# Channel mixer: weight halves meet paired columns of 512, sample tokens by gathered expert rows, lower halves of the down tiles on VectorE

## What is computed

```python
def block(xb):
    q = (xb @ w_q).reshape(blk, PEER_HEADS, 2, PEER_HALF)
    s = jnp.einsum('thcd,chkd->thck', q, sub_keys).astype(F32)
    sv, si = lax.top_k(s, PEER_TOPK)
    cand = (sv[:, :, 0, :, None] + sv[:, :, 1, None, :]).reshape(...)
    top_s, ci = lax.top_k(cand, PEER_TOPK)
    ...
    e = i1 * PEER_KEYS + i2
    gate = jax.nn.softmax(top_s, axis=-1)
    act = jax.nn.gelu(jnp.einsum('thed,td->the', u[e], xb), approximate=False)
    return jnp.einsum('the,thed->td', (gate * act), v[e])
```

## Time and profile before

| | |
|---|---|
| median of 3 runs | 2504.04 us |
| profiled execution, its span | 2507.1 us |
| first channel mixer, first to last product | 404.0 to 1268.6 us |
| second channel mixer | 1628.5 to 2493.5 us |
| TensorE busy in the span | 2330.1 us (93%) |
| VectorE, ScalarE, GpSimd busy | 1713.6, 1112.0, 1669.8 us |
| mean granted TensorE clock | 0.958 |

### The profile page before, as it was taken

How to read it: one execution, slowest core, us unless ns; L and a number is a source line. 1 busy time by engine, 2 the same in 40 slices (tenths; PEclk the granted TensorE clock), 3 DMA queues, 4 the chain that set the end, 5 groups by cost and what they waited for, 6 DMA issues and landing times. The chain is left out here.

```text
span 2507.1 us, 46304 instructions
## 1 busy us (share of the span) xinstructions
PE 2330.1 (93%) x19024; PEld 2217.5 (88%) x19024; DVE 1713.6 (68%) x2773; ACT 1112.0 (44%) x1893; POOL 1669.8 (67%) x716
## 2 busy tenths in 40 slices
PE   6977978999999999999979875899999999999998
PEld 5957858999999999999979722899999999999998
DVE  4776553795678268888868376349767762888887
ACT  4512234455554444444446412344555444444443
POOL 4714016687666788888867544758766668888885
PEclk9978988999999999999989977899999999999999
DMA  4410013454444555555535443445544445555553
GB/s 156 153 52 34 35 44 135 144 185 160 144 144 144 169 184 178 184 178 184 179 123 169 157 151 109 133 137 163 176 146 147 145 147 182 180 182 181 181 182 131
DMA packets 102226, 370.27 MB, mean 148 GB/s; under 512 B 15392, under 2 KB 15744, under 8 KB 98816
## 3 DMA queue, kind: packets, MB, share of 16 engines
q1 hardware_dynamic: 102016, 367.30, 45.4%
HBM read 352.67 MB, written 14.58 MB: 146 GB/s over the span
## 5 line engine op out<-in xcount | busy, mean ns | idle before, releaser
L355 POOL TENSOR_TENSOR weights_halves<-weights_raw,weights_halves 128x1024 fp32r<-128x1024 f32 x638 | 1541.6, 2419 | 571.1 <-ACT weights_halves L347 570.8
L347 ACT CAST weights_halves<-weights_raw 128x1024 fp32r<-128x1024 f32 x638 | 669.9, 1051 | 936.2 <-PE peer L378 482.6
L860 DVE TENSOR_TENSOR gated<-acts,gated 128x264 fp32r<-128x264 f32 x256 | 615.3, 2405 | 127.5 <-ACT gated L742 127.5
L378 PE MATMUL peer<-ffn_in_hi,weights_halves 128*128 128x264 f32 x4608 | 650.7, 288 | 14.9 <-ACT ffn_in_hi L271 14.9
L378 PEld LDWEIGHTS peer<-ffn_in_hi,weights_halves 128*128 128x128 f32 x4608 | 590.9, 189 | 22.0 <-issue 16.6
L364 PE MATMUL peer<-gated,weights_halves 128*128 128x264 f32 x2048 | 583.2, 285 | 0.0
L362 PE MATMUL peer<-gated,weights_halves 128*128 128x264 f32 x2048 | 581.2, 284 | 0.0
L363 PE MATMUL peer<-gated,weights_halves 128*128 128x264 f32 x2048 | 579.9, 283 | 0.0
L363 PEld LDWEIGHTS peer<-gated,weights_halves 128*128 128x128 f32 x2048 | 385.9, 188 | 0.0
L362 PEld LDWEIGHTS peer<-gated,weights_halves 128*128 128x128 f32 x2048 | 385.4, 188 | 0.0
L364 PEld LDWEIGHTS peer<-gated,weights_halves 128*128 128x128 f32 x2048 | 384.4, 188 | 0.0
(11 more groups left out here) (465 smaller groups left out, 2359.3 us busy)
## 6 DMA issues: line engine op xcount, KB each, us to landing
weights_raw<-in_up SPq DMA_DIRECT2D x256, 512.0 KB, 3.5
weights_raw<-in_down SPq DMA_DIRECT2D x256, 512.0 KB, 3.5
weights_raw<-in_ssm_w_in SPq DMA_DIRECT2D x40, 512.0 KB, 3.4
weights_raw<-in_w_q SPq DMA_DIRECT2D x32, 512.0 KB, 3.4
weights_raw<-in_ab_w_in SPq DMA_DIRECT2D x30, 512.0 KB, 3.5
weights_raw<-in_ssm_w_out SPq DMA_DIRECT2D x16, 512.0 KB, 3.5
states<-in_ssm_in SPq DMA_DIRECT2D x8, 1024.0 KB, 7.4
ssm_sample<-states SPq DMA_DIRECT2D x8, 1024.0 KB, 4.8
```

The costliest lines, as they stand in the source:

```text
L347: act.copy(self.halves[:, 0, slot, :], self.raw[:, slot, :]).then_inc(self.hi_made, 1)
L355: pool.tensor_tensor(self.halves[:, 1, slot, :], self.raw[:, slot, :], self.halves[:, 0, slot, :].bitcast(F32), ALU.subtract).then_inc(sel ...
L378: ins = pe.matmul(out, self.halves[:, half, n % RING, at], both[side], start=start and half == 0 and side == 0 and k == 0, stop=stop and h ...
L860: core.gated_lo.inc(dve.tensor_tensor(a_lo[:, j % RING, :], acts[:, j, :], a_hi[:, j % RING, :].bitcast(F32), ALU.subtract))
```

## The change

**512 paired columns.** The 8 sample tokens leave the up and down products, so 256 columns are left. Upper and lower token halves lie side by side (`pairs` in SBUF, `a_pairs` in the ring of gated tokens). In a down tile, and in an up tile from 40 on, an upper weight block meets all 512 columns in one matmul, and a lower one meets the 256 columns of the upper tokens and adds to the second half of the bank: 16 matmuls instead of 24. The two halves of the bank are added when they leave it: in up tiles ScalarE copies the second half to `cross`, VectorE adds it in the bank, and then comes the GELU; in down tiles VectorE adds both to `x`. Up tiles 0 to 39 keep 24 matmuls, of 256 columns. SP fills `pairs` by two DMAs from SBUF to SBUF behind the norm.

**Quads.** 64 quads instead of 66, spread over the 84 tiles 40 to 123 (`QUAD_AT`), in runs of three or four tiles with one tile between.

**Samples.** Expert numbers and gates of the samples are put on 128 rows (8 tokens x 16), one column per head. GpSimd gathers, head by head, the 128 rows of `u` (a new input `up_rows`) and then of `v` by indirect DMA into three slots. VectorE takes the dot product with the sample's row (`dot`), ScalarE one GELU, VectorE sums the weighted rows (`weigh`), all within the down tiles, one step every six tiles. 8 matmuls then sum 16 rows to a token, within the last tile.

**Lower halves.** Those of the down tiles are made by VectorE (`make_lo_on_dve`) instead of GpSimd.

```diff
+    def pair_product(self, pe, out, n, cols, pair, start, stop):
         hi, lo = self.halves[:, 0, n % RING, cols], self.halves[:, 1, n % RING, cols]
-        pe.matmul(out, hi, rhs_hi, start=start, stop=False, skip_group_check=True)
-        pe.matmul(out, hi, rhs_lo, start=False, stop=False, skip_group_check=True)
-        return pe.matmul(out, lo, rhs_hi, start=False, stop=stop, skip_group_check=True)
+        pe.matmul(out, hi, pair, start=start, stop=False, skip_group_check=True)
+        return pe.matmul(out[:, SEQ:2 * SEQ], lo, pair[:, 0:SEQ], start=False, stop=stop, skip_group_check=True)
...
-QUADS = T // 4
-EXP_TILE = 22
-TURN_TILE = 36
-FIRST_GATED = 38
-GATED_AHEAD = 120
+QUADS = SEQ // 4
+EXP_TILE = 24
+TURN_TILE = 38
+FIRST_GATED = 40
+FIRST_PAIRED = FIRST_GATED
+QUAD_TILES = 84
+GATED_AHEAD = 124
+FIRST_DOT = 10
+FIRST_WEIGHTED = 64
+SAMPLE_STEP = 6
+SAMPLES_AFTER = 3
...
@@ SP
                 core.load(sp, keys, sub_keys)
+                sp.wait_ge(core.norm_hi.sem, norm.hi0 + KC)
+                halves_paired.inc(sp.dma_start(pairs[:, :, 0:SEQ].bitcast(F32),
+                                                    h_hi[:, :, 0:SEQ].bitcast(F32)), 16)
+                sp.wait_ge(core.norm_lo_pool.sem, norm.pool0 + KC // 2)
+                sp.wait_ge(core.norm_lo_dve.sem, norm.dve0 + KC // 2)
+                halves_paired.inc(sp.dma_start(pairs[:, :, SEQ:2 * SEQ].bitcast(F32),
+                                                    h_lo[:, :, 0:SEQ].bitcast(F32)), 16)
                 ring.load_to(sp, end + RING)
@@ GpSimd
+                ring.make_lo(pool, down)
+                pool.wait_ge(core.sample_copied.sem, kinds0 + 1)
+                pool.wait_ge(ring.multiplied, down)
+                for n in range(2 * PEER_HEADS):
+                    if n >= GATHER_SLOTS:
+                        pool.wait_ge(gather_used.sem, used0 + n - GATHER_SLOTS + 1)
+                    head = n % PEER_HEADS
+                    gathered[n % GATHER_SLOTS].inc(pool.indirect_dma_start(...), 16)
                 ring.make_lo(pool, end + RING)
@@ TensorE
+                    if s == 0:
+                        pe.wait_ge(rows_copied.sem, rows_copied0 + 1)
+                        for k in range(KC):
+                            last = pe.matmul(row_banks[k // 4][:, (k % 4) * P:(k % 4 + 1) * P],
+                                             sample_rows[:, k * P:(k + 1) * P], core.ident, start=True, stop=True)
...
+                        if j == KEYS - 1 and d == SAMPLES_AFTER:
+                            pe.wait_ge(cross_added.sem, crossed0 + 4)
+                            pe.wait_ge(gather_used.sem, used0 + 2 * PEER_HEADS)
+                            for k in range(KC):
+                                summed = pe.matmul(sums[1][:, k * DEC:(k + 1) * DEC], weighted_sum[:, columns[k]],
+                                                   core.row_token, start=True, stop=True)
@@ ScalarE
                     act.wait_ge(ring.multiplied, up + j + 1)
+                    if j >= FIRST_PAIRED:
+                        cross_copied.inc(act.copy(cross, bank[:, SEQ:2 * SEQ]))
+                        ring.make_hi(act, up + j + RING + 1)
+                        act.wait_ge(halves_added.sem, added0 + j - FIRST_PAIRED + 1)
@@ VectorE
+                def add_halves(j):
+                    dve.wait_ge(cross_copied.sem, copied_cross0 + j - FIRST_PAIRED + 1)
+                    bank = projected[(SETS + j) % RING]
+                    halves_added.inc(dve.tensor_tensor(bank[:, 0:SEQ], bank[:, 0:SEQ], cross, ALU.add))
...
                 for j in range(FIRST_GATED, KEYS):
+                    quad = QUAD_AT.get(j)
+                    if j >= FIRST_PAIRED:
+                        add_halves(j)
+                    if j > FIRST_GATED:
                         gate_tile(j)
+                    if quad is not None:
+                        apply(quad, j)
+                        if quad + 2 < QUADS:
+                            build(quad + 2)
...
+                for j in range(KEYS):
+                    if j + RING < KEYS:
+                        ring.make_lo_on_dve(dve, down + j + RING)
+                        make_gated_lo(j + RING)
+                    if j >= FIRST_DOT and (j - FIRST_DOT) % SAMPLE_STEP == 0 and (j - FIRST_DOT) // SAMPLE_STEP < PEER_HEADS:
+                        dot((j - FIRST_DOT) // SAMPLE_STEP)
...
+                    add_to_x(dve.tensor_tensor(x[:, d, 0:SEQ], sums[d][:, SEQ:2 * SEQ], x[:, d, 0:SEQ], ALU.add))
+                    last = dve.tensor_tensor(x[:, d, 0:SEQ], sums[d][:, 0:SEQ], x[:, d, 0:SEQ], ALU.add)
```

More of the change, by code:

```diff
@@ L21 @@
 SSM_SLOTS = 3
+GATHER_SLOTS = 3
 class Count:
@@ L158, in _ @@
                 dve.tensor_reduce(core.sample_head, eye.rearrange("p (h t) -> p h t", t=DEC), AX_X, ALU.add)
+            dve.tensor_reduce(core.row_token, core.ident.rearrange("p (t k) -> p t k", k=TOPK), AX_X, ALU.add)
+    with nc.Block() as block:
+        @block.vector
+        def _(dve):
+            dve.tensor_scalar(core.sample_head_up, core.sample_head, float(KEYS), None, ALU.mult)
 SUM_BANK = 3
@@ L651, in score @@
                     core.head_scored.inc(last)
-                def tile_product(tile, out):
-                    ring.products(pe, out, tile, [(h_hi[:, k, :], h_lo[:, k, :]) for k in range(KC)],
-                                  [slice(k * P, (k + 1) * P) for k in range(KC)], start=True,
-                                  stop=True, norm=norm if tile == first else None).then_inc(ring.multiplied, 1)
+                columns = [slice(k * P, (k + 1) * P) for k in range(KC)]
                 for s in range(SETS):
@@ L672, in _ @@
                         pe.wait_ge(core.tile_gated.sem, gated0 + j - RING - FIRST_GATED)
-                    tile_product(up + j, projected[bank][:, 0:T])
+                    if j == 0:
+                        pe.wait_ge(halves_paired.sem, paired0 + 32)
+                    if j < FIRST_PAIRED:
+                        last = ring.products(pe, projected[bank][:, 0:SEQ], up + j,
+                                             [(pairs[:, k, 0:SEQ], pairs[:, k, SEQ:2 * SEQ]) for k in range(KC)],
+                                             columns, start=True, stop=True)
+                    else:
+                        last = ring.pair_products(pe, projected[bank][:, :], up + j,
+                                                  [pairs[:, k, :] for k in range(KC)], columns)
+                    last.then_inc(ring.multiplied, 1)
                     if j == 0:
@@ L2847, in program @@
             sources += [d[name][n] for n in tiles]
-        core.ring = Ring(core, ctx, sources)
+        on_dve = {first[name] + j for name in ("down0", "down1") for j in range(KEYS)}
+        core.ring = Ring(core, ctx, sources, on_dve)
         with nc.Block() as block:
```

226 lines of the change are left out of this document (159 added, 67 removed).

## The result

The changed kernel takes 2463.5 us (median of 4 runs, 2462.8 to 2466.1); before, on the same chips, 2506.2. The ratio is 0.9832, its 95% interval 0.9818 to 0.9846: 42.7 us faster, where 74 were forecast. The time lies within the range on record (2400 to 2474), and outside the likeliest case's own range (2408 to 2450).

What follows compares the result with a forecast made beforehand. TensorE was taken as the bound, through the distance between matmul starts. Tile and quad savings of -96 us, +8 for the round, +13 for mixer starts and ends and +1 summed to -74: 2430 us, range 2400 to 2474.

Steps and rivals of the forecast that it cites:

- likeliest case: Whole kernel: TensorE sets the pace throughout, 2430 us, own range 2408 to 2450; chance 0.52.
- the hidden loads: Rival, paired tiles: all weight loads hide, a tile takes 2.62 us, the whole 2410 or 2403; chance 0.08.
- the round: Paired up tiles: VectorE and ScalarE waiting on each other, about 3.85 us a tile with a quad; term +8 us (0 to +40).
- tiles of 2.8 us without a wait: Paired tiles: sign that the working is wrong and the matmul's loss grows with its columns.
- the price of the 512-column matmul: Paired up and down tiles: 0.216 us, of which 0.213 is columns; with a 256-column matmul 0.337 a pair.
- Down tiles: 256 down tiles in both mixers, from 2.915 to 2.70 us each: -55 us (-22 to -76).
- Paired up tiles: 176 up tiles, 40 to 127 of both mixers, from 2.90 to 2.70 us each: -35 us (-12 to -49).
- Start and end of the mixers: Each mixer: sample-row matmuls 1.8 us, a late weight load 0.5, its end 4.4; +13 us for both.
- The loss goes with the columns: Rival, paired tiles: the matmul's loss scales with columns, a tile takes 2.83 us, the whole 2480; chance 0.10.
- The round sets the up tiles: Rival, paired up tiles: VectorE and ScalarE's chain binds; 2454 us at 0.3 us more a round, 2479 at 0.5; chance 0.25.
- Lower halves take 2.4 us: Rival, down tiles: VectorE's lower halves take as long as beside GpSimd, 2.40 us; the whole 2536; chance 0.04.
- the end: End of a mixer: two dependent additions a bank, TensorE stopping until the first four are added: +4.4 us a mixer (2 to 7).

Runs made afterwards that it cites:

- p1: Changed kernel plus a stage behind its end, TensorE running rows of 96 matmuls of one kind: fp32r 512 columns 0.226 us, 256 columns 0.120, a pair alone 0.354.
- e1: Changed kernel with unpaired down tiles, three matmuls of 256 columns a block and one addition per bank at the end: 2476.9 us.
- e2: Changed kernel with one quad on every up tile from 40 to 103, instead of 64 on 84 tiles: 2500.3 us.
- e3: Changed kernel with the last down tile unpaired, second halves added meanwhile, and each sample matmul behind its block: 2457.9 us.
- e4: Changed kernel with the down tiles' lower halves back on GpSimd, the gathers queued between them: 2585.9 us.
- e6: Changed kernel with down tiles' lower halves on GpSimd, gathers queued late enough to find their slots free, first three halves ahead of the first gathers: 2518.8 us.
- e5: Changed kernel without pairs in the up tiles, so no copy of cross columns and no addition there: 2476.6 us.
- p2: Changed kernel plus rows mixing types behind its end, TensorE alone: a block of one fp32r and two bf16 products 0.355 us product by product, 0.345 sorted by type.

## Why the prediction was right, and where it was off

**The forecast held, but not by its mechanism.** The range was drawn to hold the likeliest case, the hidden loads and most of the round, and none of these is what happened; that the time falls into it is luck of a wide range. By its own signs ("tiles of 2.8 us without a wait") the working was wrong.

**The step that was off is the price of the 512-column matmul**, put at 0.216 us ("next to nothing is added" where the stream is longer than a load). It was read off fp32 matmuls, whose stream is as long. p1 shows that both rows were right and the transfer wrong: fp32 pays 2.5 ns, fp32r 13 at any length above a load's 0.11 us. In a row of its own it costs 0.226 us, 10 ns more than forecast, and the 256-column one 0.120, 1.5 less than forecast; with the 4 ns of a pair that stay open, a pair is 0.350 in the kernel, not 0.337. Over 432 tiles of eight pairs these 13 ns are 45 us.

**Terms of the sum**, forecast and measured, from the distances of tiles. Down tiles -55, and 256 x (2.915 - 2.80) = -29. Paired up tiles -35, and 176 x (2.90 - 2.79) = -19. Up tiles 0 to 39 -3, and 80 x (2.90 - 2.88) = -2. Two quads fewer -3 and -3. The round +8 and about 0. Start and end of the mixers +13, and 2 x (1.3 + 4.3) = +11. The extra block at the start +1, not read by itself. Sum -74 and -42.

**The rivals.** "The loss goes with the columns" came nearest in the tile (2.83 us; 2.80 measured), though its time, 2480, is 16 us too long, and its mechanism is wrong: e1 has the same columns and loses 13 us. "The round sets the up tiles" did not come true: its 3.85 us are real (e2), and TensorE, slower than forecast, hides them. VectorE's timeline of the changed kernel has both kinds of round, 3.89 us with a quad and 1.41 without:

```profile
699.33 0.84 DVE L979 TENSOR_TENSOR acts<-peer,acts 128x288 f32<-128x288 f32 x1 [0.24 <-ACT acts L902]
...
703.22 0.84 DVE L979 TENSOR_TENSOR acts<-peer,acts 128x292 f32<-128x292 f32 x1 [0.23 <-ACT acts L902]
...
705.69 0.43 DVE L973 TENSOR_TENSOR peer<-peer,cross 128x256 f32<-128x256 f32 x1
...
707.10 0.43 DVE L973 TENSOR_TENSOR peer<-peer,cross 128x256 f32<-128x256 f32 x1 [0.21 <-ACT cross L890]
```

16 x 3.89 + 5 x 1.41 = 69.3 us in 21 tiles. TensorE needs 70.8 there; at the 69.0 that the forecast gave it, the round would have become the bound by a hair (worked out, not run). "All loads hide" (0.328 a pair) is excluded by p1's 0.346 to 0.354. "Lower halves take 2.4 us" is excluded by L391's 1.23; the price forecast was 1.22.

**Right in size, wrong in working: the end.** +4.4 a mixer was forecast, +4.3 measured (from the start of the last tile to that of the last square 10.5 us instead of 6.2). That the two agree is luck. TensorE waits for two banks to be added, not for four as the prediction read the code, since each bank counts twice in the semaphore (idle 0.72 us instead of 2.4); the samples' matmuls take the 1.8 us forecast; and the fall of the clock, which nobody reckoned with, costs 4 x (0.64 - 0.35) = 1.2 us in the pairs and about half a microsecond in the squares.

**Hidden as forecast:** gathers, dot products and weighting; TensorE's one wait in the down tiles is the 0.72 us at the end.

## What to carry to other kernels

Price a matmul by a row of its own type: another type of the same stream length said nothing. When a stage has no waits, more columns per instruction save only the fixed price of each instruction left out (in fp32r 10 ns in this kernel and 13 in rows of one kind, in bf16 3), and a change of type may save more than a longer instruction. Where a helper engine has 15% of a stage to spare, ask what stands behind a short step in its queue, and what the two engines do to each other, before adding one to either.

## What was not expected of the hardware

At 1.2 GHz the fixed price is gone: pairs start 0.64 us apart, which is 768 columns by the clock. In p1 the clock fell in the midst of matmuls that follow each other without a gap: in a row of 96 with 64 columns the granted clock is 0.50 (first stretch below) and they start 0.21 us apart instead of 0.111.

What brings the clock down at the end of a mixer is only partly shown. In e3 the same sixteen eight-column instructions, behind the same wait but spread between longer ones, left it at 1.00. In e1 they follow each other as in the changed kernel, but without a wait ahead of them, and it stays at 1.00 too (second stretch). So neither the wait nor the sixteen did it alone in these runs. Both together did not always do it either: in both mixers of e4 (third stretch, behind a wait of 0.71 us) and in the first of e6 the clock stayed, while it fell in both mixers of the changed kernel, of e2 and of e5. Why is open.

```profile
2615.00:2625.00 10.00, 10.00 (x49) 10.00 (x48) 0.00 (x0) 0.00 (x0) 0.00 (x0) 0.50 0.01 2
...
1253.00:1255.00 2.00, 2.00 (x17) 1.93 (x17) 1.77 (x8) 1.61 (x6) 0.54 (x1) 1.00 0.00 0
...
1304.00:1306.00 2.00, 2.00 (x12) 1.72 (x11) 1.90 (x6) 1.72 (x6) 0.00 (x0) 1.00 0.00 0
```

Why fp32r pays 13 ns where fp32 with the same bytes pays 2.5, and why a change between fp32r and bf16 costs 12 ns in p1 (0.024 us for two) and some 6 in p2 (0.355 against 0.343 by the rows apart, for two), stays open: the runs give the prices, not the mechanism.
